# Splitting small matmuls of a hybrid decoder layer into strips of 32 on TensorE

## What is computed

```python
x = x + mix @ w_out[l]                # mix: GLA heads (A) and gated DeltaNet heads (B)
hn2 = rmsnorm(x, norm2_g[l])
up, ffn_new = causal_dwconv(hn2 @ w_up[l], st_ffn[l], ffn_conv_w[l])
a_f, b_f = jnp.split(up, [D_FF], axis=-1)
x = x + (jax.nn.silu(a_f) * b_f) @ w_down[l]
```

## Time and profile before

| what | value |
|---|---|
| median of 3 runs | 3509.62 us (3505.3 to 3510.6) |
| profiled execution, own time | 3505.47 us |
| its span in the profile | 3503.8 us |
| mean granted clock of TensorE | 0.989 |
| TensorE busy (matmul) | 3413.8 us, 97% |
| VectorE busy | 2078.9 us, 59% |
| ScalarE, GpSimd busy | 894.0 us, 559.4 us |
| mixer's part, MLP's part | up to about 1795 us, and the rest |

### The profile page before, as it was taken

One profiled execution on the slowest core, in us unless ns is written; L12 is line 12 of the kernel. 1 busy time (PEld: TensorE's weight loads), 2 busy tenths in 40 slices (PEclk: granted clock), 3 DMA queues, 4 the chain that ended last, 5 costly groups with the idle time before them and its releaser, 6 DMA issues. The chain is left out here.

```text
span 3503.8 us, 47709 instructions
## 1 busy us (share of the span) xinstructions
PE 3413.8 (97%) x16065; PEld 2376.7 (68%) x16065; DVE 2078.9 (59%) x4728; ACT 894.0 (26%) x1880; POOL 559.4 (16%) x825
## 2 busy tenths in 40 slices
PE   7999999999999999999889999999998999999998
PEld 3666666666666666666567777777767887778775
DVE  2556665555566555556435666566677666666667
ACT  2222333232233322222312121212132222222223
POOL 1111110111111011111213112111134111211110
PEclk9999999999999999999889999999999999999999
DMA  6012212211222121112551111111124111111112
GB/s 225 25 61 78 78 61 77 66 60 55 71 78 78 60 78 59 45 54 67 169 159 37 49 36 48 36 48 48 47 81 146 37 37 42 44 49 37 37 37 73
DMA packets 225002, 233.98 MB, mean 67 GB/s; under 512 B 14204, under 2 KB 169380, under 8 KB 224883
## 3 DMA queue, kind: packets, MB, share of 16 engines
q1 hardware_dynamic: 224883, 232.42, 21.3%
HBM read 202.71 MB, written 29.67 MB: 66 GB/s over the span
## 5 line engine op out<-in xcount | busy, mean ns | idle before, releaser
L610 PE MATMUL mixer_bank<-arena,hnt 128*128 128x451 f32 x2176 | 913.9, 549 | 21.5 <-DMA arena<-in_w_in_dram 12.0
L1861 PE MATMUL mlp_bank<-arena,ws 128*128 128x176 f32 (+1 forms) x3520 | 659.3, 340 | 11.7 <-ACT raw L2041 7.1
L1861 PEld LDWEIGHTS mlp_bank<-arena,ws 128*128 128x128 f32 x3520 | 589.7, 191 | 50.7 <-ACT raw L2041 9.0
L610 PEld LDWEIGHTS mixer_bank<-arena,hnt 128*128 128x128 f32 x2176 | 386.1, 191 | 316.6 <-issue 309.7
L1933 PE MATMUL mlp_bank<-arena 128*128 128x512 f32 x1120 | 493.7, 592 | 0.0
L2306 DVE TENSOR_TENSOR acc<-acc,mlp_bank 128x512 f32<-128x512 f32 x560 | 370.4, 685 | 57.2 <-PE mlp_bank L1933 54.4
L1933 PEld LDWEIGHTS mlp_bank<-arena 128*128 128x128 f32 x1120 | 211.2, 190 | 231.7 <-issue 205.2
L2273 DVE SCALAR_TENSOR_TENSOR mcv<-raw,cf,mcv 128x512 f32<-128x512 f32 (+2 forms) x440 | 285.8, 666 | 60.9 <-ACT mcv L2014 50.5
L565 POOL TENSOR_TENSOR ex<-dtt,level 128x512 f32<-128x512 f32 (+1 forms) x114 | 143.3, 1257 | 1067.1 <-DVE dtt L1445 715.6
L991 ACT ACTIVATE proj<-mixer_bank,x_rs 128x451 f32<-128x451 f32 x136 | 86.5, 636 | 727.0 <-PE mixer_bank L610 726.8
L1861 PE MATMUL mlp_bank<-arena 128*128 128x176 f32 (+1 forms) x1320 | 254.8, 343 | 10.9 <-POOL ident_mlp L2180 10.0
(11 more groups left out here) (332 smaller groups left out, 3940.9 us busy)
## 6 DMA issues: line engine op xcount, KB each, us to landing
wo<-in_w_out_dram SPq DMA_DIRECT2D x272, 256.0 KB, 2.9
arena<-in_w_up_dram SPq DMA_DIRECT2D x44, 512.0 KB, 5.0
wu<-in_w_up_dram SPq DMA_DIRECT2D x44, 512.0 KB, 5.0
arena<-in_w_down_dram SPq DMA_DIRECT2D x40, 512.0 KB, 4.1
arena<-in_w_in_dram SPq DMA_DIRECT2D x8, 1804.0 KB, 17.1
xc<-in_x_t_dram SPq DMA_DIRECT2D x16, 512.0 KB, 3.9
xt<-in_x_prompt_dram SPq DMA_DIRECT2D x16, 512.0 KB, 4.9
xr<-in_x_prompt_dram SPq DMA_DIRECT2D x16, 512.0 KB, 3.5
```

Of the source, the lines that this page charges most:

```text
L610: x = pe.matmul(bank[ring(g)][0:N, 0:GW], hnt[:, k, 0:N], w[:, k, g * GW:(g + 1) * GW], start=(k == 0), stop=(k == KT - 1))
L1861: x = pe.matmul(out[:, 0:N], left[:, k, :], xb[:, slot, k, g * N:(g + 1) * N], start=first and k == 0, stop=k == HK - 1, skip_group_check= ...
```

## The change

The level products are written in strips of 32 keys, each with only the queries of its own blocks; three levels make a round (`ROUND = 3`), so there are three rounds in place of four. Banks 5 and 7 are cleared once at the start.

```diff
-ROUNDS = (NL + 1) // 2
+ROUND = 3
+ROUNDS = (NL + ROUND) // ROUND
...
+        def strips(l, N):
+            if l == NL:
+                return [(slice(k, k + S), slice(k, k + S), slice(k, k + S)) for k in range(0, N, S)]
+            span = SPANS[l]
+            if span < S:
+                return [(slice(k, k + S), slice(k, k + S), slice(k // 2, k // 2 + S // 2)) for k in range(0, N, S)]
+            return [(slice(k + i, k + i + S), slice(k + span, k + 2 * span), slice(k // 2, k // 2 + span))
+                    for k in range(0, N, 2 * span) for i in range(0, span, S)]
...
-                    if a >= 2 and a % 2 == 0:
-                        fill(*((9, 16) if sample else ((9, 11), (11, 13), (13, 16))[a // 2 - 1]))
-                        pe.wait_ge(s_at_level, (NL + 1) * t + a)
-                    for h in range(H):
...
+                    if a % ROUND == 0:
+                        if a:
+                            fill(*((9, 12), (12, 16))[a // ROUND - 1])
+                            pe.wait_ge(s_at_level, (NL + 1) * t + a)
...
+                    for g, (keys, queries, cols), e in every(range(2), strips(l, N), range(2)):
+                        out = level_out(a, l, e, N)[keys, g, cols]
+                        r = slice(64 * e, 64 * e + 64)
...
+                            x = pe.matmul(packed(out, l), ke[r, l, g, keys], blocks(qe[r, l, g, queries], l, 1),
+                                          start=True, stop=True)
```

```diff
+                def block_products(a, l, out, left, right, r, N):
+                    if N < C or not 1 < a < NL - 2:
+                        return pe.matmul(packed(out[:, 0:N // 2], l), left[:, 0:N], blocks(right[:, 0:N], l, r),
+                                         start=True, stop=True)
+                    for b in range(4):
+                        k = slice(S * b, S * b + S)
+                        x = pe.matmul(packed(out[k, 16 * b:16 * b + 16], l), left[:, k], blocks(right[:, k], l, r),
+                                      start=True, stop=True)
+                    return x
...
-                    if a >= 2:
+                    if a == NL - 1:
                         for h in range(H):
                             x = pe.transpose(heads(4)[0:N, h, 0:N], xi[0:N, h, 0:N], ident[0:N, 0:N])
...
+                    if 0 < a and not last:
+                        for h in range(H):
+                            x = block_products(a, l, heads(3)[0:N, h], xit[0:N, h], new[0:N, h], 0, N)
+                    if turned_later:
+                        x.then_inc(s_dx_done, 1)
+                        fill(23 + 2 * a, 24 + 2 * a)
+                        continue
                     for h in range(H):
...
+                        if a:
+                            x = block_products(a, l, heads(4)[0:N, h], new[0:N, h], xit[0:N, h], 1, N)
```

```diff
-        OUTS = (28, 30)
+        OUTS = (28, 29)
...
                 if ps and half and last >= 14:
+                    bank_free(ps, i, 28)
                     for e in range(2):
-                        bank_free(ps, i, 28 + e)
-                        plain(bank[4 + e], 2 * p, wd, 8, e, S)
+                        for j in range(2):
+                            r = slice(64 * e + S * j, 64 * e + S * j + S)
+                            x = pe.matmul(bank[4][r, :], act_[2 * p + j][:, T // 2:T // 2 + S],
+                                          wd[j][:, e * 512:e * 512 + 512], start=True, stop=True)
+                    x.then_inc(s_down_done, 1)
...
             def plain(out, a, right, t, e, N):
+                if t == 8:
+                    pe.matmul(out[0:N, :], fold[:, e, :], y_parts[:, :], start=True, stop=False)
```

More of the change, by code:

```diff
@@ L18 @@
 from functools import partial
+from itertools import product as every
 import concourse.bass as bass
@@ L562, in mixer @@
                 for a, l in enumerate(inv):
+                    turned_later = not sample and a == NL - 2
                     gp.wait_ge(s_lt_made, n)
@@ L567, in mixer @@
                         .then_inc(s_ltm_made, 1)
-                    if a in (0, len(inv) - 1):
+                    if not turned_later:
                         if a >= 2:
@@ L709, in mixer @@
+                    if a % ROUND == ROUND - 1 or l == NL:
                         x.then_inc(s_at_done, 1)
-                fill(16, 18)
+                fill(9 if sample else 16, 18)
                 pe.wait_ge(s_conv_sq, n)
@@ L802, in mixer @@
                         if a:
-                            x = pe.matmul(packed(heads(5)[0:N, h, 0:N // 2], l), ltm[0:N, h, 0:N],
-                                          blocks(xi[0:N, h, 0:N], l, 0), start=True, stop=True)
+                            x = block_products(a, l, heads(5)[0:N, h], ltm[0:N, h], xi[0:N, h], 0, N)
                         else:
@@ L817, in mixer @@
                     pe.wait_ge(s_p_out, NL * t + a + 1)
-                    if a == 0 or last:
-                        pe.wait_ge(s_pp_cleared, 2 * t + last + 1)
+                    turned_later = a == NL - 2
+                    if not turned_later:
+                        pe.wait_ge(s_pp_cleared, (NL - 1) * t + a + (a < NL - 1))
                     pe.wait_ge(s_xit_new, NL * t + a)
-                    for h in range(H):
[L822 to L827, removed]
+                    if 0 < a and not last:
[5 more added lines that the diff above has]
+                        continue
+                    for h in range(H):
+                        if a:
+                            x = block_products(a, l, heads(4)[0:N, h], new[0:N, h], xit[0:N, h], 1, N)
                         else:
@@ L1526, in mixer @@
                             .then_inc(s_xi_new, 1)
-                    if a and last:
+                    if a and a != NL - 2:
                         v = blocks(xit[0:N, :, 0:N], l, 1)
@@ L2181, in _ @@
                              pattern=[[-1, C]], channel_multiplier=1).then_inc(s_ident_made, 1)
+            gp.memset(y_parts[:, :], 0.0).then_inc(s_parts_cleared, 1)
+            gp.wait_ge(s_ident_made, 2)
+            halves = ident[:, :].rearrange("p (e j i) -> p e j i", e=2, j=2)
+            gp.tensor_tensor(fold[:, :, :], halves[:, :, 0, :], halves[:, :, 1, :], ALU.add).then_inc(s_fold_made, 1)
             for ps in range(2):
@@ L2305, in down @@
                         dve.wait_ge(s_y_added, n + o)
-                    dve.tensor_tensor(v, v, bank[4 + o % 4][0:S if o >= 28 else C, :], ALU.add).then_inc(s_y_added, 1)
+                    dve.tensor_tensor(v, v, bank[4 + o % 4][:, :], ALU.add).then_inc(s_y_added, 1)
             def combine(ps, n, q0, q1, steps):
@@ L2349, in close @@
                         v = half_acc(t, e, N)
-                        dve.tensor_tensor(v, v, bank[4 + o % 4][0:N, :], ALU.add).then_inc(s_y_added, 1)
+                        if t == 8:
+                            dve.tensor_copy(v, bank[4 + o % 4][0:N, :]).then_inc(s_y_added, 1)
+                        else:
+                            dve.tensor_tensor(v, v, bank[4 + o % 4][0:N, :], ALU.add).then_inc(s_y_added, 1)
                         o += 1
```

62 lines of the change are left out of this document (37 added, 25 removed).

## The result

The changed kernel takes 3535.1 us (median of 4 runs, 3529.3 to 3538.7) against 3508.3 (3505.3 to 3510.6): a ratio of 1.0075, 95% interval 1.0058 to 1.0093. It is slower by 0.75% where 3468 was forecast. The profiled run took 3529.3 us.

A forecast was written before the change was run, and what follows sets the result against it. TensorE's own instructions, in their order, were taken to set the time (97% busy). From 3505.5 us, -26 - 3 - 46 - 3 - 25 + 1.7 - 1 + 43 + 22 = -37 gave 3468 us; range 3400 to 3600.

The forecast's parts named there:

- 2, 3 inverse: Mixer's inverse: levels 2 to 4 in strips save 0.95 us, 48 times, -46; levels 1 and 5 together -3.
- 1 levels and rounds: Mixer's level products: strips save 1.63 us a tile, -26; three rounds in place of four, -3.
- 1 waits for VectorE behind the rounds: Mixer's level products: VectorE's six copies behind each round are covered by the longer fills, 0.
- sample's tile; start: Sample's tile loses a 1.5 us wait, -1 as VectorE is late next; added starting memsets and fold cost 0.
- 4 sample's down-projection: MLP: eight instructions in four column groups take 1.0 us instead of 3.55, ten times, -25; closing fold +1.7.
- 5 mixer's jumps and clock: Mixer's longer loop: 13 jumps cost 3.3 us more each, +43, and half clock behind them 1.7 each, +22.
- step 5: Code length: the mixer's loop, grown to some 1770 instructions, no longer fits, +43 and +22; MLP jumps stay hidden.
- C (15 ns): Rival for strips in mixer and MLP: only two instructions run side by side, 15 ns a strip; 3535 us, chance 0.20.
- D (30 ns): Rival, inverse levels 2 to 4: strips of different columns wait for each other, 30 ns each; 3621 us, chance 0.18.
- E (25 ns floor): Rival for levels and inverse: a floor of 25 ns under each instruction however short; 3606 us, chance 0.04.
- Rival B: Mixer's jump stays at 0.2 us because the longer code still fits; 65 less, 3403 us, chance 0.14.
- 1602 don't fit: MLP's second loop: its 1602 instructions are fetched again each pass, jump 3.3 to 3.7 us; used against the short-jump rival.

The follow-up runs named there:

- e3: Only the inverse's three middle levels in strips, level products and MLP as in the kernel before: 3469.5 us, ratio 0.9891.
- e13: The kernel before with only the sample's down-projection in the MLP in strips: 3484.8 us, ratio 0.9938.
- e2: Only the level products in strips with three rounds, inverse and MLP as in the kernel before: 3492.4 us, ratio 0.9955.
- e4: The changed kernel with the last two fill parts directly ahead of the mixer's jump and turn_mixed(1) behind it: 3451.3 us, ratio 0.9838.
- e9: e4 with fill part 20 (two long matmul calls) ahead of gla_out() instead of behind it: 3435.8 us, ratio 0.9793.
- e14: The kernel before with 97 semaphore increments at the start of TensorE's program: 3509.7 us, ratio 1.0009.
- e7: The changed kernel with spans 32, 64 and the diagonal as whole products again, strips in the rest: 3496.0 us.
- e8: e7 with 100 semaphore increments at the very start of TensorE's program: 3460.1 us.
- e5: The changed kernel with 96 semaphore increments on TensorE's queue ahead of the MLP's second loop: 3512.2 us.
- e10: e4 with 66 semaphore increments at the start of TensorE's program: 3428.0 us, ratio 0.9770.

## Why the prediction was wrong

Against the profiled execution of before, the change measured out as follows (us; a pass times 16 tiles where a tile is meant).

| step | forecast | measured |
|---|---|---|
| 2, 3 inverse | -49 | -37 (e3: 2.3 a pass) |
| 1 levels and rounds | -29 | -32 |
| 1 waits for VectorE behind the rounds | 0 | +16 |
| sample's tile; start | -1 | +2 |
| 4 sample's down-projection | -23 | -2 in place (-21 in e13) |
| 5 mixer's jumps and clock | +65 | +77 |
| sum | -37 | +24 |

(The mixer's part ends where the MLP waits for its identity: at 1804.9 us before, 1767.8 in e3, 1790.8 in e2, 1830.8 in the changed kernel, 1752.7 in e4. So e3 is worth -37 and e2 -14, and +77 is the changed kernel's +26 less these two; e4 gives 78 for the same. e2's -14 splits by its timeline: the rounds of a tile with the fills between them take 15.83 us in place of 17.82, two waits behind them 1.0 more; the +2 is what is left over.)

- **The step that failed** is in step 5: "In the MLP the long matmuls in the queue hide the jump", priced 0. It was read from the earlier trace rows, where the products that the change removes were themselves the cover, and where the next block of code came in time. Both were taken as fixed. The lost cover cost 1.4 us a pass, 4 in all; the second wait for code 5.8 a pass, 17 in all, since the loop was moved by edits in another stage. The forecast named no such effect. It is the largest of four errors that make up the 61 us between the sums; without it alone the changed kernel would have come out level with the one before, still not 1% faster.
- **"VectorE's six copies behind each round are covered by the longer fills"** failed too, and cost 16 us. Two copies stand ahead of gla_out(): from L755 to L768 TensorE takes 1.30 us, before 0.67. And L742, which by the kernel waits for ScalarE's squares of VectorE's convolution, starts some 0.25 us later behind its fill than before, and the work behind it takes 0.10 more, in every tile. For gla_out() e9 shows it; the second wait is read from the timelines, no run took it out.
- **Prices.** A strip is 10 to 10.5 ns and not 8. The bursts of a level of the inverse take 1.04 us for 96 instructions, 0.77 forecast; the long work beside them takes 0.33 us more, near the 0.4 taken. So a level saves 0.75 us and not 0.95, which is 10 of the 12 us missing in the inverse. Rivals C (15 ns), D (30 ns) and E (25 ns floor) are out. C's sum of 3535 met the result by accident: its strips at 15 ns didn't happen.
- **The mixer's jumps** were right in mechanism and length (3.3 to 3.9 us, 13 times; 44 us idle against 43). The fall of the clock was priced from one stretch of 3.4 us; in 5 of 13 it lasted about 10. That accounts for the +77 against +65: 5 x (10 - 3.4)/2 = 16.
- **Rival B** (only blocks count, and the loops differ in place) was half right: the place does decide, but 1838 instructions are more than 7 blocks of 256 wherever they lie.
- "1602 don't fit" was the wrong reading of the earlier trace rows: this same loop jumps in 0.2 us in e3 and e14. The Trainium skill (Runtime: NRT & Kernel Launch, Instruction fetch mechanics) has blocks and a window that a jump must stay in. That is nearer to what the runs show than the forecast's length limit, though by the count at e7 some 7 blocks stayed and not the 8 that the page's 2048 instructions make, and e8's four long jumps fit neither.

## What to carry to other kernels

When an edit makes a loop longer, count its instructions on the busiest engine and look at the time of its jump back and at the instruction packets inside it; then look at what stands in the queue ahead of the jump. If it is short work, or work behind a late semaphore, move a long fill there: that cost nothing here and gave back some 80 us. And an edit moves all code behind it: a loop in another stage can gain or lose 20 us by place alone, so compare the jump rows of every loop, not only of the one that was edited. Where padding is tried, place it beside a wait that hides it, and judge by the passes and not by the total.

## What the runs showed of the hardware

- MATMUL instructions of f32 strips of 32 columns, spread over four column groups, follow each other every 10 to 10.5 ns in bursts of 64 and 96, each with its own weight load beside it.
- A loop of one and the same 1693 to 1695 instructions jumps in 0.21 us or in 3.3 to 3.8, by its place in the code. In one place TensorE then idles 5.0 to 5.7 us (changed kernel), in another 1.2 and 0.4 (e13); that a second block of code is missed there is argued.
- Behind a pause of 3.1 to 3.7 us TensorE mostly runs at half clock: for 3.4 us in some cases, for up to 10 in others, in the same kernel at the same instruction, and in one case of e8 not at all. So a pause of 3.7 us cost up to 8.4 us. That is the source of the run-to-run scatter of the changed kernel.
- Semaphore increments in a row on TensorE's queue go out every 0.15 us: 96 in 14.7 us (e5), 97 in 14.7 (e14), 100 in 15.1 (e8). Beside the wait for the first weights, 66 cost nothing (e10) and 97 delay the first matmul by 4 us (e14).
